# A hybrid attention and expert layer: stick-breaking sums by a scan instead of a triangular product

## What is computed

```python
# stick-breaking: a[t,s] = sigmoid(z_ts) * prod_{s<j<t} (1 - sigmoid(z_tj)), s < t
z = einsum('bhqd,bhkd->bhqk', qi, k) * scale
causal = key_pos[None, :] < q_pos[:, None]
log_keep = where(causal, -softplus(z), 0.0)
tail = cumsum(log_keep, axis=3, reverse=True) - log_keep
a = where(causal, exp(log_sigmoid(z) + tail), 0.0)
out = einsum('bhqk,bhkd->bhqd', a, v)
...
h = x + (sigmoid(g_sb) * (y_sb @ w_proj_sb) + sigmoid(g_mb) * (y_mb @ w_proj_moba)) @ w_out
hn = rmsnorm(h, norm_ffn_g)
logits = hn @ w_router + b_router          # top 4 of 32, softmax over them
for each expert:
    hgu = hn @ w_gate_up + b_gate_up
    gate, up = minimum(hgu[:, :1024], 7), clip(hgu[:, 1024:], -7, 7)
    acc += gates[:, e] * (((up + 1) * gate * sigmoid(1.702 * gate)) @ w_down + b_down)
out = rmsnorm(h + acc, norm_final_g)
```

## Time and profile before

| | us |
|---|---|
| median of 3 runs | 1134.65 |
| lowest and highest | 1134.47, 1135.13 |
| the profiled execution's own time | 1134.32 |
| its span in the profile | 1132.6 |
| TensorE busy in the span | 1073.5 |
| VectorE, ScalarE, GpSimd busy | 259.9, 151.1, 122.2 |

### The profile page before, as it was taken

How to read it: one execution, slowest core, us unless ns; L and a number is a source line. 1 busy time by engine, 2 the same in 40 slices (tenths; PEclk the granted TensorE clock), 3 DMA queues, 4 the chain that set the end, 5 groups by cost and what they waited for, 6 DMA issues and landing times.

```text
span 1132.6 us, 14442 instructions
## 1 busy us (share of the span) xinstructions
PE 1073.5 (95%) x6022; PEld 451.5 (40%) x6022; DVE 259.9 (23%) x482; ACT 151.1 (13%) x315; POOL 122.2 (11%) x140
## 2 busy tenths in 40 slices
PE   8999999999999999999999999999999999999986
PEld 7676444633434333333333333333333333333322
DVE  2345756621111111111111112111210111111112
ACT  2233222320000000000000001000100000000002
POOL 1357592400000000000000000000000000000000
PEclk9999999999999999999999999999999999999999
DMA  9943238899999999999999999999999999999996
GB/s 321 346 184 150 88 136 352 353 370 428 426 428 435 427 428 428 431 429 432 429 432 435 428 429 435 427 429 433 434 428 429 432 433 428 432 426 428 426 424 255
DMA packets 36705, 437.30 MB, mean 386 GB/s; under 512 B 4488, under 2 KB 5568, under 8 KB 16992
## 3 DMA queue, kind: packets, MB, share of 16 engines
q1 hardware_dynamic: 34752, 435.44, 91.5%
q10 hardware_dynamic: 1920, 1.39, 0.5%
HBM read 435.76 MB, written 1.06 MB: 386 GB/s over the span
## 4 chain that ended last, share of the span: by engine, by line
PE 56%; DMA 40%; DVE 2%; issue 1%; ACT 0%; SPq 0%; POOL 0%; POOLq 0%
DMA ring<-in_w_down_dram 29%; PE bank L1905 19%; PE bank L1942 13%; DMA ring<-in_w_gate_up_dram 11%; PE bank L1583 9%; PE bank L1567 5%; PE bank L1878 2%; PE bank L1872 2%; PE bank L1933 1%; PE bank L1667 1%; PE bank L1893 0%; PE bank L1927 0%; PE bank L1692 0%; DMA resid<-in_x_dram 0%; PE bank L1527 0%
## 5 line engine op out<-in xcount | busy, mean ns | idle before, releaser
L1905 PE MATMUL bank<-ring,gates 128*64 128x512 f32 x2048 | 472.2, 604 | 16.8 <-DMA ring<-in_w_gate_up_dram 16.8
L1942 PE MATMUL bank<-ring,gates 128*64 128x512 f32 x1008 | 225.5, 595 | 26.1 <-DMA ring<-in_w_down_dram 25.9
L1905 PEld LDWEIGHTS bank<-ring,gates 128*64 128x64 f32 x2048 | 139.2, 138 | 261.8 <-issue 230.8
L1415 DVE TENSOR_SCALAR gates<-bank 128x512 f32<-128x512 f32 x31 | 21.4, 692 | 709.4 <-PE bank L1905 709.4
L1942 PEld LDWEIGHTS bank<-ring,gates 128*64 128x64 f32 x1008 | 71.1, 137 | 175.5 <-issue 140.2
L709 POOL COPY expert_sel<-expert_row 96x64 bf16 x32 | 7.5, 233 | 843.7 <-PE bank L1872 838.1
L619 POOL TENSOR_TENSOR ring<-ring 128x512 f32<-128x512 f32 x60 | 82.6, 1409 | 67.0 <-DVE ring L1072 34.9
L1872 PEld LDWEIGHTS bank<-onehot,qkT 128*128 128x128 bf16 x1488 | 52.2, 118 | 25.2 <-issue 25.2
L1878 PE MATMUL bank<-gates,scatter_w 64*128 64x512 f32 x248 | 61.6, 615 | 0.0
L929 ACT ACTIVATE gates<-gates 128x512 f32<-128x512 f32 x32 | 20.2, 630 | 279.4 <-DVE gates L1415 279.2
L1872 PE MATMUL bank<-onehot,qkT 128*128 128x64 bf16 x1488 | 55.5, 198 | 0.0
(11 more groups left out here) (257 smaller groups left out, 646.9 us busy)
## 6 DMA issues: line engine op xcount, KB each, us to landing
ring<-in_w_gate_up_dram SPq DMA_DIRECT2D x44, 4096.0 KB, 28.1
ring<-in_w_down_dram SPq DMA_DIRECT2D x59, 2048.0 KB, 21.1
ring<-in_w_gate_up_dram SPq DMA_DIRECT2D x39, 2048.0 KB, 14.4
ring<-in_w_in_dram SPq DMA_DIRECT2D x9, 2048.0 KB, 15.4
ring<-in_w_down_dram SPq DMA_DIRECT2D x7, 1024.0 KB, 25.4
ring<-in_w_out_dram SPq DMA_DIRECT2D x2, 2048.0 KB, 8.7
ring<-in_w_in_dram SPq DMA_DIRECT2D x4, 512.0 KB, 7.3
ring<-in_w_proj_sb_dram SPq DMA_DIRECT2D x1, 2048.0 KB, 7.9
```

The costliest lines, as they stand in the source:

```text
L1415: V.tensor_scalar(gate_t, bank[4][:, :], SWIGLU_LIMIT, None, ALU.min).then_inc(gate_rd, 1)
L1905: ins = mm(bank[4 + i][SLOTS * c:SLOTS * (c + 1), :], xe[:, k, :], ring[:, base + k // 2, n0:n0 + CH], start=False, stop=k == KD - 1)
L1942: ins = mm(bank[to][SLOTS * c:SLOTS * (c + 1), :], rows, ring[:, place, j * D + c * CH:j * D + (c + 1) * CH], start=k == 0, stop=k == KD - 1)
```

## The change

1. **Stick-breaking pairs.** The scores lie with queries on the partitions, as in MoBA pairs. `stick_sum` computes softplus, then a scan along the keys (backwards, starting anew at the ends of the rows through the factors in `restart`), then scores minus sum; ScalarE's exp gives the weights, one mask (GpSimd) follows, and `middle` transposes them. `neg_tri` and `keep_masks` go. GpSimd's order changes, and on VectorE `stick_sum` moves ahead of one unit's read, for pair 3 ahead of units 14 and 15.
2. **Token sums of the mixers.** `mixed` makes `S1` to `S4` from the bank and what it has copied; `left_sums(MIX_SB)` and `moba_sum` go.
3. **MoBA probabilities** are scaled on ScalarE; the maximum comes negated out of the reduction.
4. **Before the experts.** All residual copies on ScalarE; GpSimd makes the third piece of the first 128 tokens and the first `expert_sel` early; the first gather goes in two halves to banks 7 and 6, and expert 0 starts on the first.
5. Several semaphores are merged.

```diff
@@ GpSimd
+            link(nc.gpsimd.memset(restart[:, :], 1.0))
...
-            keep_masks(0)
+            weight_masks(0)
+            weight_masks(1)
             for h in range(2):
                 pool.wait_ge(gate_in[0][h], 16)
-            weight_masks(0)
             first_sums(GATE_SB)
-            keep_masks(1)
...
+            weight_masks(2)
             second_sums(GATE_SB)
-            weight_masks(1)
             third_sums(GATE_SB)
-            keep_masks(2)
+            weight_masks(3)
...
+            nc.gpsimd.tensor_tensor(pieces[2][:, 0, :], res2[0], pieces[1][:, 0, :], ALU.subtract).then_inc(third_p, 1)
+            nc.gpsimd.tensor_copy(expert_sel[:, :], expert_row[:, 0:1].to_broadcast([3 * E, SLOTS])).then_inc(sel_rd, 1)
@@ ScalarE
+                    for b in range(2):
+                        act.wait_ge(below_rd, 2 * p + b + 1)
+                        nc.scalar.activation(att_s[:, b, :], att_s[:, b, :], ACT.Exp).then_inc(weight_raw, 1)
...
+                            nc.scalar.activation(att_s[:, b, c0:c1], att_s[:, b, c0:c1], ACT.Copy,
+                                                 scale=rr[:, b, q:q + 1]).then_inc(prob_rd, 1)
@@ VectorE, stick_sum
-                    V.scalar_tensor_tensor(out=att_s[:, b, :], in0=z_bank[(2 * p + b) % 4][:, 0:TRI], scalar=0.0,
-                                           in1=att_e[:, b, :], op0=ALU.max, op1=ALU.add).then_inc(softplus, 1)
+                    link(V.scalar_tensor_tensor(out=att_s[:, b, :], in0=z, scalar=0.0, in1=att_e[:, b, :], op0=ALU.max,
+                                                op1=ALU.add))
+                    V.tensor_tensor_scan(att_a[:, b, ::-1], restart[:, ::-1], att_s[:, b, ::-1], 0.0, ALU.mult, ALU.add
+                                         ).then_inc(suffix_rd, 1)
+                    dve.wait_ge(suffix_rd, 2 * p + b + 1)
+                    V.tensor_tensor(att_s[:, b, :], z, att_a[:, b, :], ALU.subtract).then_inc(below_rd, 1)
@@ VectorE, mixed
-                V.tensor_copy(yT[:, pair, :], o_bank[pair % 2][:, 0:T]).then_inc(pv_rd, 1)
+                copied = V.tensor_copy(yT[:, pair, :], o[:, 0:T])
+                if pair % SB_PAIRS < 2:
+                    link(copied)
+                    V.tensor_tensor(s3, o[:, 0:P], yT[:, pair, P:T], ALU.subtract).then_inc(pv_rd, 1)
+                else:
...
+                    V.tensor_tensor(s1, o[:, P:T], yT[:, pair - 2, P:T], ALU.add)
+                    link(V.tensor_tensor(s2, o[:, P:T], s3, ALU.subtract))
+                    V.tensor_tensor(s4, o[:, 0:P], s2, ALU.subtract).then_inc(pv_rd, 1)
@@ VectorE, order
             for p in (1, 2):
-                later_units(range(3 * p + 5, 3 * p + 7))
+                later_units(range(3 * p + 5, 3 * p + 6))
                 stick_sum(p)
-                later_units(range(3 * p + 7, 3 * p + 8))
+                later_units(range(3 * p + 6, 3 * p + 8))
...
+            stick_sum(3)
             later_units(range(14, 16))
-            stick_sum(3)
             mixed(2)
@@ TensorE, middle
-                        mm(z[:, 0:TRI], neg_tri[:, :], a[:, :], start=False, stop=True, skip_group_check=True)
-                        ins = mm(z[:, P:T], neg_one[:, :], a[:, T:TRI], start=False, stop=True, skip_group_check=True)
+                        pe.wait_ge(weights_rd, 2 * p + b + 1)
...
+                    for i in range(3):
+                        ins = tp(z[:, i * P:(i + 1) * P], a[:, i * P:(i + 1) * P], ident[:, :])
@@ TensorE, first_gather
+                for h in range(2):
+                    tokens(0, 0, h, piece_rd, 1)
+                    tokens(0, 1, h, piece_rd, 2)
+                    tokens(0, 2, h, third_p, 1)
+                    tokens(1, 0, h, piece_rd, 3 + h)
+                    tokens(1, 1, h, piece_rd, 5 + h)
+                tokens(1, 2, 0, third_rd, 1).then_inc(gathered_low, 1)
+                ins = tokens(1, 2, 1, third_rd, 2)
```

More of the change, by code:

```diff
@@ L304, in hybrid_layer @@
         ln_rd = sem("ln_rd")
-        softplus = sem("softplus")
-        keep_rd = sem("keep_rd")
+        suffix_rd = sem("suffix_rd")
+        below_rd = sem("below_rd")
         mid_ps = sem("mid_ps")
@@ L602, in mask @@
                 nc.gpsimd.affine_select(out=diagonal(t), in_=diagonal(t), compare_op=ALU.is_gt, fill=0.0, base=0,
[L603 to L608, removed]
+                                        pattern=[[0, 2], [-1, P]], channel_multiplier=1).then_inc(ready, 1)
             def weight_masks(p):
@@ L704, in _, with experts @@
             left_over(0, 0, slice(0, D), 1)
-            left_over(1, 0, slice(0, D), 2)
-            def experts(done):
-                with pool.Fori(0, E) as e:
+            pool.wait_ge(piece_rd, 2)
+            nc.gpsimd.tensor_tensor(pieces[2][:, 0, :], res2[0], pieces[1][:, 0, :], ALU.subtract).then_inc(third_p, 1)
+            nc.gpsimd.tensor_copy(expert_sel[:, :], expert_row[:, 0:1].to_broadcast([3 * E, SLOTS])).then_inc(sel_rd, 1)
+            def experts(done, start=0):
+                with pool.Fori(start, E) as e:
                     pool.wait_ge(gathered, e + (done + 1))
@@ L710, in experts @@
                                           ).then_inc(sel_rd, 1)
-            experts(0)
+            experts(0, 1)
             more_passes(pool, lambda r: experts(r * E), most_tokens(pool))
@@ L814, in _ @@
                                                  ).then_inc(prob_raw, 1)
+                    for b in range(2):
+                        act.wait_ge(even_rd, 2 * (p - SB_PAIRS) + b + 1)
+                        for q, (c0, c1) in enumerate(((0, P), (P, TRI))):
+                            nc.scalar.activation(att_s[:, b, c0:c1], att_s[:, b, c0:c1], ACT.Copy,
+                                                 scale=rr[:, b, q:q + 1]).then_inc(prob_rd, 1)
                 if p == 0:
@@ L1388, in weigh @@
                 return most_tokens(dve)
-            def start_rows(n):
-                V.tensor_copy(bank[n][:, :], resid[:, n // 2, n % 2 * CH:(n % 2 + 1) * CH]).then_inc(start_rd, 1)
             def one_hots(col):
@@ L1453, in experts @@
                 if r is None:
-                    left_over(1, 5)
-                    third_piece(0, 6)
-                    third_piece(1, 7)
-                next_tokens(0, done)
-                if r is None:
+                    left_over(1, 4)
+                    third_piece(0, 5)
+                    third_piece(1, 6)
+                    first_tokens(0, bank[7], gathered_low, xe_low)
+                    first_tokens(1, bank[6], gathered, xe_rd)
                     count()
-                    start_rows(2)
+                else:
+                    next_tokens(0, done)
                 one_hots(1).then_inc(onehot_rd, 1)
```

182 lines of the change are left out of this document (74 added, 108 removed).

## The result

| | before | after |
|---|---|---|
| median | 1134.58 us | 1136.62 us |
| lowest and highest of 22 runs each | 1133.83, 1135.17 | 1135.61, 1138.29 |
| the profiled execution: own time, span | 1134.32, 1132.6 | 1137.77, 1135.9 |

The ratio is 1.0020, with a 95% interval from 1.0015 to 1.0026. The kernel became 2.0 us slower where the forecast had it 0.9 us faster. The spread grew too, from 1.3 to 2.7 us.

The account below looks back on a forecast made before the run. From about 229 us the DMA weight stream bounds the kernel, before that TensorE; -3.4 (three savings) + 6.6 (P1 wait) - 1.1 - 1.3 - 1.7 = -0.9 us, from 1134.65 to 1133.8 us, range 1130.0 to 1137.3.

Parts of the forecast that it names:

- VectorE's schedule: VectorE between the units, 76.2 us on: stick_sum 4.1 us instead of 1.0, unit 14 read at 104.9.
- the two turns with GpSimd that I took: Before unit 14's read, VectorE waits for GpSimd: up to three turns of 1.1 us, two counted, 2.2 us.
- Rival 1: VectorE quicker, scans 0.51 us and no GpSimd turns: P1 near 101.0, kernel 1129.9 to 1132 us; chance 0.21.
- rival 2: No TensorE wait at P1, the change does all it seems to: -7.5, 1127.2 us; chance 0.06.
- `P1` starts 3.3 us later than before: GATE_SB's first product on TensorE waits 6.6 us for unit 14's read, after three savings, and starts at 104.9.
- The fourth `middle` gives back 1.1: +2.2 us when the MoBA scores start: After P1, pair 3's cheaper middle saves 1.1 us on TensorE, leaving the MoBA scores 2.2 us later than before.
- The MoBA part: Both TensorE waits for VectorE's last_rows (1.04 and 0.25 us) go: -1.3 us, bounds 0 and -1.3.
- the bounds are -0.5, if TensorE's half slot sets it, and -1.7: Before the experts: residual copies ending earlier start the weight stream sooner relative to this part; -1.7 us taken.
- rival 4: TensorE's half slot starts the stream, so the copies' gain is lost: 1135.0 us; chance 0.56 together with the forecast.
- The prediction's own sign of being wrong: Weight stream in the experts: a DMA stream not at 430 GB/s after 236 us would show the forecast wrong.
- That load is 1 MB, 2.4 us at 430 GB/s: Load of resid's place at the experts' start: next load issued 2.4 us behind it, so the stream starts 1.7 us sooner.
- rival 3: VectorE and GpSimd turns cost all they can before unit 14: P1 at 108.2, kernel 1137.1 us; chance 0.17.

Follow-up runs that it names:

- experiment 6: Residual copies as before the change (three on ScalarE, last on VectorE): on the changed kernel 1135.34 us, repeat without it 1136.18; on the kernel with the third move 1127.63.
- experiment 4: Changed kernel with twelve idle products on TensorE ahead of the wait for unit 14: 1134.49 us, ratio 1.0000 to the kernel before.
- Experiment 5: Kernel before, with extra maxima on VectorE ahead of the read of unit 14: six 1143.22 us, three 1138.51 us.
- the third move: Changed kernel, unit 14 read first, pair 3's masks early, plus last_bias_part's last two passes moved behind unit 15's read: 1128.12 us, repeat 1129.40.
- experiment 1: Changed kernel with unit 14 read ahead of stick_sum(3) on VectorE, unit 15 behind it: 1133.18 us, ratio 0.9983 to the kernel before.

## Why the prediction was wrong

**VectorE's schedule was right.** Alone, `stick_sum` takes 4.1 us (85.00 to 89.1), the scan 0.96 (0.93 forecast, at the upper bound). The Trainium skill's half throughput for the scan ("DVE: opcode table, instruction layouts, handler registers and perf-mode slots", Datapath and trigger behaviour) points the same way as the trace, which shows less than a halving: 0.96 us against the 0.56 of a plain pass, 1.7 times as long. `last_bias_part` starts at 89.88 and `stick_sum(3)` at 98.76, 0.6 later than forecast each. Of the two turns with GpSimd that I took one came, 2.01 against 0.96; in the version with unit 14 first two came, with the masks first none. The Trainium skill's rule that the loser blocks for a whole instruction ("SBUF — State Buffer", Who interferes with whom) now has its rows for a scan: the blocked one takes 1.05 us more, where one of GpSimd's sums takes 1.25 to 1.27 undisturbed. In each profile of the changed order the first scan of pair 3 runs beside the same sums in 0.96 us, so the cost depends on how the two engines happen to meet. (The prediction counted the tensor_scalar of the earlier trace rows as agreeing with the rule; it has only one input in SBUF, so the rule as quoted there does not cover it.) `P1` started at 104.46, 0.45 sooner than forecast. Rival 1 (under 3 us of wait) and rival 2 fell.

**The step that failed first: "`P1` starts 3.3 us later than before" was taken for the whole price of the wait.** "The fourth `middle` gives back 1.1: +2.2 us when the MoBA scores start": it was +4.62. The sum counted TensorE's idle time and let the work behind it run at full pace. The clock fell to 0.50 within the wait, and eight products took 2.9 us more in the profiled execution, 2.6 and 1.7 in two others (experiment 6); on the medians it is up to 2.1 (experiment 4). Experiment 5 shows the same price in the kernel before, 2.8 us.

**The MoBA part: right, a little too small.** From the scores to the product behind the last transposes of this part 4.62 became 2.81 (the product that starts at 164.88 before starts at 167.69 now): -1.8 us where -1.3 was forecast. The two waits are gone, and the other 0.5 is theirs too: all other rows in between are spaced alike, and the kernel before loses 1.30 us around the wait printed as 1.04 and 0.51 around the one of 0.25. The wait of 2.27 in experiment 5 moved the scores by 2.56. So each of these waits costs about a quarter of a microsecond more than its bracket, even at full clock.

**The second step that failed: "the bounds are -0.5, if TensorE's half slot sets it, and -1.7", of which I took -1.7.** TensorE's own tail gained 0.8 (2.81 to 2.02 us), and the stream went with TensorE's slot: the five loads behind the first landed 1.1 to 1.9 us later than before, though the first one landed only 0.6 us later. That is rival 4. But even its price was too kind: the early copies cost 0.8 us beside the old ones on the medians, about 1 us in the profiles (experiment 6). The copies themselves came as forecast: they end 0.84 us later than before where TensorE, at 164.88, was 2.81 later, so 2.0 us sooner against it (1.7 forecast). The prediction's own sign of being wrong, a stream that is not at 430 GB/s after 236 us, showed: it was 396. "That load is 1 MB, 2.4 us at 430 GB/s" reckoned that the queue filled earlier is the stream moved earlier; the stream then ran below that rate for 24 us.

**The sum again.** The forecast was -0.9. The clock +2.1; the last part -0.8 + 0.8 = 0.0 instead of -1.7, so +1.7; ahead of that `P1` 0.45 sooner and the MoBA part 0.5 better, -1.0. Together +1.9 us; measured +2.0. In the profiled executions, with 2.9 for the clock and 1.3 for the stream, the same list gives +3.2, measured +3.3. That the two lists close is no proof of each term; the clock's on the medians may be 1.3 to 2.1. The range held the time, but by luck: its upper end stood for rival 3, which gave nearly this time (1137.1) by a mechanism that did not come. Of the turns that it counts one was there.

**What the change could have been worth.** With unit 14 read first and pair 3's masks ahead of the last sums the kernel takes 1129.2 us, and with the old copies and the third move 1127.6. That is about rival 2's time (1127.2), though not by its terms. The last kernel starts the MoBA scores 3.9 us sooner than the kernel before (4.5 in the rival), gains another 2.6 up to expert 0 (1.3 in the rival), and 0.5 in the stream (1.7 in the rival, for the copies). So the passes saved on TensorE were real, and the changed kernel lost nearly all of them to the order of the work on VectorE and GpSimd.

## What to carry to other kernels

A wait on TensorE amid dense work cost more than its length here, 0.3 us at full clock and 1.6 to 2.9 us in the profiles where the clock fell: add what the next products take at half the clock, and ask of each wait that a change makes whether one result can be handed over earlier or the gap filled. When work moves from TensorE to an engine with little slack, first look at what stands behind the new passes in that engine's order; here moving one read and two masks brought 7.4 us (1136.62 to 1129.19). A load that could go out earlier did not help here, since the load behind it did not move.

## What was unexpected of the hardware

- The granted clock fell to 0.50 within a wait of 5.61 us, and in the kernel before within one of 5.64 too. The moment differs: in three profiles with this wait TensorE had idled for 2.2, 4.0 and 4.5 us when it fell, and the eight products behind took 5.33, 6.23 and 6.51 us. Behind 2.25 us it was 0.50 in one profile (experiment 1) and behind 2.27 us 1.00 in another (experiment 5). With 24 products that nobody reads in the gap it stayed 1.00.
- The runs of the changed kernel spread by 2.7 us, those of the kernel before by 1.3. The moment of the fall can be a part of this, but not all: with the clock kept at 1.00 they spread by 2.25 us (experiment 4), and the kernel before by 2.15 in another 21 runs (1133.50 to 1135.65).
- The same scan takes 0.96 or 2.01 us, and a plain pass 0.56 or 1.67, beside GpSimd's sums; 1.39 and 1.79 occur as well.
- The stream's rate from 236 to 260 us depends on how the loads start, 396 and 410 GB/s against 428 and 430, at a DMA share of 0.99 to 1.01 in all. The cause is open.
